# A two-layer hybrid decoder step with hierarchical experts: the experts' rows scattered through DRAM instead of brought back by matmuls

## The chip, the cores and the metric

One NeuronCore of a Trainium2 chip runs the whole step. The metric is the device time of one execution in microseconds.

## The reference

288 tokens (256 of a new sequence, 32 of eight running ones) of width 1024 go through two layers. Of each layer the first half (RG-LRU, Conformer convolution and retention groups, an output projection) isn't touched by the change. The second half is the mixture of experts: each token picks one of 4 groups and in it 2 of 8 experts, so 2 of 32 experts, with a gate for each.

```python
def hier_moe(x, wg, bg, we, be, w1, w3, w2):
    ...
    gates = jnp.sum(jax.nn.one_hot(eid, N_EXPERTS) * (p_top * pe)[..., None], axis=1)
    def expert(acc, params):
        w1e, w3e, w2e, ge = params
        h = jax.nn.silu(xt @ w1e) * (xt @ w3e)
        return acc + ge[:, None] * (h @ w2e).astype(jnp.float32), None
    y, _ = lax.scan(expert, jnp.zeros((B * T, D), jnp.float32), (w1, w3, w2, gates.T))
```

All is float32. An expert's w1, w3 (1024 x 256) and w2 (256 x 1024) are 1 MB each, so a layer reads 96 MB of expert weights. 288 tokens with 2 experts each make 576 rows of 4 KB.

## The kernel before, in words

Every engine has its own program; semaphores alone order them. The experts of a layer are handled in 16 pairs. Each expert has 64 slots for tokens; a pair fills 128 partitions. Before the experts a routing stage works out, for each slot of each pair, which token sits there (`gidx`), its gate (`sel`) and, as `selu`, the number 2 x token + choice; an empty slot has a number past the bound. More tokens than 64 for one expert would go to overflow blocks behind the stage (the `If(n > 0)` parts).

**Weights.** `ring` has 12 places of 1 MB, three (w1, w3, w2) for each of four experts, that is for two pairs. SP issues the loads: `expert` (L473, w1, and L474, w3) once the up projection of the expert two pairs back is done, `expert2` (L478, w2) once the down projection two pairs back is done. The last expert of a layer has places of its own (`spare_w1` and so on, L516 and L521), filled ahead of the stage. SP's instructions go in order, and its loads share one DMA queue.

**A pair on TensorE** (`experts4`): `up` (L918) of the first expert, 32 matmuls into one bank; `turn_h` (L570), two transposes of the hidden rows that ACT has copied out; `up` and `turn_h` of the second; `tokens` (L570), eight transposes of the gathered rows of the next pair; `down` (L944), 16 matmuls into the two banks y0 and y1. ACT makes the tanh and, in `results` (L1850), takes y0 and y1 out, scaled by the gates, into `ysb`. DVE multiplies the hidden values (L1551, L1553) and applies the norm's weights to the turned tokens (L1543).

**Way back.** The rows in `ysb` belong to tokens all over x. POOL builds a matrix of zeros and ones (`back`, L1969), DVE splits `ysb` into three bfloat16 parts (L1561, L1564), and TensorE multiplies: `give_back` (L957, L966, L972) has five parts, two halves of each of the two 128-token tiles and one of the 32 samples, in banks 6 and 7. DVE adds each to x (L1573, L1577). This is done for every pair, between the steps of the next one. For the last pair it stands behind the stage, and then x's norm starts the next layer (or the final norm).

**Gathers.** POOL fetches the token rows of pair g + 1 from the DRAM copy `xn_scratch` by an indirect DMA (L1960) into one of two buffers, once the transposes have read the one before; rows past the bound are skipped.

**Next layer.** SP loads w_in (L493) into the ring's places as the last pairs free them.

## Time and profile before

| | us |
|---|---|
| median of 3 runs | 947.17 |
| lowest, highest | 943.45, 955.58 |
| the profiled execution's own time | 946.95 |
| its span | 945.1 |
| TensorE busy in it | 871.9 (92%) |
| DVE, ACT, POOL busy | 538.7, 173.5, 133.2 |
| DMA moved | 252.79 MB |

The profile is of one execution, in microseconds from the start of its span. A pair of experts takes 15.69 us; the expert stage of layer 0 lies between about 210 and 471 us, that of layer 1 between about 677 and 938 us. PE is TensorE's matmuls, PEld its weight loads. SPq and ACTq are DMA issues of these engines.

### The profile page before, as it was taken

To read this page: it belongs to the slowest core of one execution; us is meant where nothing else is said; L and a number is where in the kernel's file an instruction comes from. 1 tells how busy PE (TensorE), PEld (TensorE's weight loads), DVE (VectorE), ACT (ScalarE), POOL (GpSimd) and SP (SyncE) were. 2 spreads that over 40 slices of the span, in tenths; PEclk is the share of its full clock that TensorE was granted. 3 is DMA by queue.
4 is the path that set the end of the run, shared out by engine and by line. 5 is a ranking of instruction groups with operands and counts; after the bars stand their busy time and mean duration, and the time that the engine had idled before them with its cause. 6 is when DMAs were issued, how large, how long until landed. Compare 5 with 4: busy or idle time off the path is not lost.

```text
span 945.1 us, 14840 instructions
## 1 busy us (share of the span) xinstructions
PE 871.9 (92%) x5548; PEld 493.5 (52%) x5580; DVE 538.7 (57%) x1205; ACT 173.5 (18%) x357; POOL 133.2 (14%) x217
## 2 busy tenths in 40 slices
PE   7999969979999999999799996998799999999994
PEld 6744524575555555555376444336655555555551
DVE  2378794362656565656625787834445555555556
ACT  2213111101211111111301221212012111111113
POOL 0101120031212121211010001200411212121100
PEclk9999979999999999999999998799999999999998
DMA  9953704368999999992953055225499999999911
GB/s 294 309 204 135 232 22 130 133 220 351 409 383 414 404 409 402 419 409 115 345 190 133 1 226 134 89 51 226 162 395 394 418 414 418 407 406 387 391 69 51
DMA packets 100881, 252.79 MB, mean 267 GB/s; under 512 B 31682, under 2 KB 65494, under 8 KB 84438
## 3 DMA queue, kind: packets, MB, share of 16 engines
q1 hardware_dynamic: 73502, 239.45, 65.8%
q10 hardware_dynamic: 22728, 8.02, 3.7%
q0 software_dynamic: 4608, 4.73, 1.6%
q8 instruction: 28, 0.46, 0.2%
q14 instruction: 15, 0.12, 0.0%
HBM read 258.13 MB, written 6.52 MB: 280 GB/s over the span
## 4 chain that ended last, share of the span: by engine, by line
PE 73%; issue 14%; DVE 7%; ACTq 2%; DMA 1%; POOL 1%; ACT 1%; DVEq 0%; SPq 0%; POOLq 0%
PE psum L918 24%; PE psum L944 12%; PE psum L639 10%; PE psum L618 7%; PE psum L570 5%; PE psum L972 4%; PE psum L966 3%; DVE x L1573 3%; ACTq L1783 2%; DVE cb L1193 2%; PE psum L957 2%; PE psum L650 1%; PE psum L576 1%; DMA rows<-xn_scratch,sg 1%; PE psum L713 1%
## 5 line engine op out<-in xcount | busy, mean ns | idle before, releaser
L918 PE MATMUL psum<-ring,arena 128*64 128x256 f32 x1984 | 229.5, 384 | 2.4 <-DVE arena L1543 2.4
L918 PEld LDWEIGHTS psum<-ring,arena 128*64 128x64 f32 x1984 | 143.0, 138 | 87.4 <-issue 25.9
L1573 DVE TENSOR_TENSOR x<-x,psum 128x512 f32<-128x512 f32 x128 | 82.2, 684 | 160.6 <-PE psum L972 160.4
L944 PE MATMUL psum<-ring,arena 128*64 128x512 f32 x496 | 116.8, 598 | 2.4 <-DVE arena L1553 2.4
L639 PE MATMUL psum<-ring,uT 128*128 128x512 f32 x256 | 114.4, 601 | 0.0
L1969 POOL TENSOR_SCALAR kT<-const,sg 128x128 bf16<-128x128 f32 (+1 forms) x96 | 49.2, 522 | 360.9 <-PE psum L957 360.7
L639 PEld LDWEIGHTS psum<-ring,uT 128*128 128x128 f32 x256 | 48.6, 193 | 56.6 <-issue 55.5
L1561 DVE TENSOR_TENSOR v<-arena 128x512 f32<-128x512 f32 x64 | 44.3, 692 | 45.8 <-ACT arena L1850 45.7
L1850 ACT ACTIVATE arena<-psum,sg 128x512 f32<-128x512 f32 x64 | 44.0, 687 | 136.4 <-PE psum L944 136.4
L1857 ACT ACTIVATE arena<-psum 128x256 f32<-128x256 f32 x64 | 24.5, 383 | 238.2 <-PE psum L918 238.2
L944 PEld LDWEIGHTS psum<-ring,arena 128*64 128x64 f32 x496 | 34.2, 136 | 60.7 <-issue 57.3
L618 PE MATMUL psum<-uT,ring 128*128 128x288 f32 x256 | 63.1, 407 | 1.0 <-DVE uT L1118 1.0
L831 PE MATMUL psum<-ring,mixT 128*128 128x512 f32 x128 | 59.5, 620 | 3.3 <-DVE mixT L1409 3.2
L570 PE MATMUL psum<-const,rows 128*128 128x128 f32 (+1 forms) x352 | 49.4, 284 | 9.2 <-DMA rows<-xn_scratch,sg 4.6
L618 PEld LDWEIGHTS psum<-uT,ring 128*128 128x128 f32 x256 | 48.2, 190 | 14.2 <-DVE uT L1118 1.3
L1193 DVE SCALAR_TENSOR_TENSOR cb<-glp,prm,cb 128x256 f32<-128x256 f32 x120 | 54.8, 531 | 0.5 <-DVE hst L1322 0.4
L1577 DVE TENSOR_TENSOR x<-x,psum 32x256 f32<-32x256 f32 x128 | 52.9, 413 | 1.5 <-issue 0.2
L570 PEld LDWEIGHTS psum<-const,rows 128*128 128x128 f32 (+1 forms) x352 | 42.6, 193 | 18.4 <-issue 7.1
L972 PE MATMUL psum<-v,kT 128*128 128x512 bf16 x128 | 49.5, 387 | 1.9 <-DVE kT L1564 1.9
L972 PE MATMUL psum<-kT 128*128 128x512 bf16 x128 | 48.3, 377 | 0.0
L1543 DVE TENSOR_TENSOR arena<-psum,gff 128x512 f32<-128x512 f32 x64 | 41.2, 686 | 12.0 <-PE psum L570 11.1
L576 PE MATMUL psum<-const 128*128 128x128 f32 x282 | 37.8, 299 | 6.9 <-DMA const<-in_constants 4.6
(279 smaller groups left out, 872.1 us busy)
## 6 DMA issues: line engine op xcount, KB each, us to landing
ring<-in_moe_w SPq DMA_DIRECT2D x186, 1024.0 KB, 9.4
ring<-in_w_in SPq DMA_DIRECT2D x24, 1024.0 KB, 11.9
ring<-in_w_out SPq DMA_DIRECT2D x8, 1024.0 KB, 6.4
arena<-in_state_ret ACTq DMA_DIRECT2D x16, 128.0 KB, 8.4
out<-arena ACTq DMA_DIRECT2D x16, 128.0 KB, 2.5
xn_scratch<-rows ACTq DMA_DIRECT2D x4, 512.0 KB, 5.8
uT<-in_moe_w SPq DMA_DIRECT2D x2, 1024.0 KB, 9.8
mixT<-in_moe_w SPq DMA_DIRECT2D x2, 1024.0 KB, 12.7
```

Of the source, the lines that this page charges most:

```text
L570: return pe.transpose(out, in_, ident[0:n, 0:n])
L576: pe.matmul(b[:, 0:128], ident, ident)
L618: i = pe.matmul(b, w[:, k, 128 * (c % 2):128 * (c % 2) + 128], uTk[:, k, :], start=k == 0, stop=k == KT - 1)
L639: i = pe.matmul(b, uTk[:, k, 128 * t:128 * t + 128], w[:, :, k, :], start=k == 0, stop=k == KT - 1)
L831: i = pe.matmul(b, mixT[:, k, 128 * t:128 * t + 128], w[:, :, k, :], start=n_ == 0, stop=n_ == KT - 1)
L918: i = pe.matmul(b[64 * j:64 * j + 64, 0:FE], xsT[:, u // 2, k, s], w[j][:, k, :], start=k == 0, stop=k == KT - 1, skip_group_check=True)
L944: i = pe.matmul(b[64 * q:64 * q + 64, :], hT[:, q, f, :], w[:, 512 * j:512 * j + 512], start=f == 0, stop=f == 1, skip_group_check=True)
L972: i = pe.matmul(b, back[:, pair, 64 * (a - a % 2):64 * (a - a % 2) + 128], y[:, 512 * (a % 2):512 * (a % 2) + 512], start=False, stop=y is ...
L1193: chain[c] = own(STT(dst, glp[:, c, k:k + SEQ], w, dst, ALU.mult, ALU.add))
L1573: i = T(s, s, psum[:, b, :], ALU.add)
L1577: i = T(s, s, psum[32 * q:32 * q + 32, b, 0:256], ALU.add)
L1969: own(pool.tensor_scalar(back[:, g % 2, o:o + n], C("iota")[:, 0:n], tok[:, t, g:g + 1], None, ALU.is_equal))
```

## The change

Let g be the pair's number, 0 to 15.

- The rows of pairs 0 to 13 (`VIA_DRAM`) are written by an indirect DMA from POOL (`scatter`) to `y_dram`, a DRAM scratch of 576 rows, row 2 x token + choice; empty slots are skipped. The scratch is zeroed in each layer by one DMA from SP, whose source is one 512-column row on 64 partitions that POOL has set to zero, read 18 times each.
- When all 14 scatters have landed, SP reads the scratch back in three DMAs (2.36 MB in all) into places 9 to 11 of the ring, both rows of a token side by side. POOL adds the two rows, DVE adds the sum to x (`sums`).
- Pairs 14 and 15 go by `give_back` still, but both accumulate in the same five banks (6, 7, 0, 1, 2), and DVE adds them once at the end (`given_back`).
- On TensorE the down projection of pair g - 1 stands behind the first up projection of pair g (`experts2`); ACT takes its results out there, after waiting for the scatter of pair g - 2 to have landed, since `ysb` is one buffer.
- SP issues the w2 loads of pair p - 1 between the w1 and w3 loads of the two experts of pair p, after a wait for the down projection of pair p - 3. Places 9 to 11 are given to the next layer's w_in only after DVE's sums.
- POOL issues gather g + 2 and then scatter g.

```diff
+VIA_DRAM = NPAIR - 2
...
-EXPERT_TURN = [2, 2, 4, 4, 2, 2, 6, 4]
-PER_BANK = [n + GROUPS * k for n, k in zip(PER_BANK, EXPERT_TURN)]
+EXPERT_TURN = [2, 2, 4, 4, 2, 2, 0, 0]
+BACK_BANK = [6, 7, 0, 1, 2]
+PER_BANK = [n + GROUPS * k + BACK_BANK.count(b) for b, (n, k) in enumerate(zip(PER_BANK, EXPERT_TURN))]
...
+    y_dram = nc.dram_tensor("y_scratch", (2 * NT, D), F32, kind="Internal").ap()
...
+                        if g >= 9:
+                            sp.wait_ge(sums_added, 3 * (l - 1) + g - 8)
+                        elif g % 3 == 2:
+                            xfull(sp, "y1", g // 6, GROUPS - 1, l - 1)
                         else:
-                            xfull(sp, "h", g // 3, last_turn, l - 1)
+                            xfull(sp, "h", g // 3, GROUPS - 1, l - 1)
                     elif g == 10:
...
                     sp.dma_start(spare_w2[f], w2[l, NE - 1, 128 * f:128 * f + 128, :]).then_inc(spare2_in, 16)
-                for it in range(1, GROUPS):
-                    for pair in range(2):
-
-                        experts = [u for u in (2 * pair, 2 * pair + 1) if 4 * it + u < NE - 1]
-                        for u in experts:
-                            xfull(sp, "h", u, it - 1, l)
-                            expert(l, it, u)
-                        xfull(sp, "y1", pair, it - 1, l)
...
+                    pair, it = pair_of(p)
+                    a, b = 2 * pair, 2 * pair + 1
+                    xfull(sp, "h", a, it - 1, l)
+                    expert(l, it, a)
+                    if p > 2:
+                        xfull(sp, "y1", *pair_of(p - 3), l)
+                        late = pair_of(p - 1)
+                        for u in (2 * late[0], 2 * late[0] + 1):
+                            expert2(l, late[1], u)
+                    if 4 * it + b < NE - 1:
+                        xfull(sp, "h", b, it - 1, l)
+                        expert(l, it, b)
+                xfull(sp, "y1", *pair_of(NPAIR - 3), l)
+                expert2(l, GROUPS - 1, 2)
+
+                sp.wait_ge(scattered, 16 * VIA_DRAM * (l + 1))
+                for t, (o, n) in enumerate(TILES):
+                    sp.dma_start(ring[0:n, 9 + t, :].rearrange("p (k d) -> p k d", k=2),
+                                 y_dram.rearrange("(t k) d -> t k d", k=2)[o:o + n]).then_inc(sums_in[t], 16)
                 sp.wait_ge(idx_ready, l + 1)
...
+                def give_back(last, parts):
+
+                    turn_ = 2 * l + last
...
-                def experts4(it, first=False, last=False):
-                    for pair in range(2):
-                        before = (0, it) if pair else (1, it - 1)
-                        up(2 * pair, it)
-                        if pair or not first:
-                            give_back(*before, (0, 1))
-                        turn_h(2 * pair, it)
-                        up(2 * pair + 1, it, spare=last and pair == 1)
-                        if pair or not first:
-                            give_back(*before, (2, 3))
-                        turn_h(2 * pair + 1, it)
-                        if pair or not first:
-                            give_back(*before, (4,))
-                        if not (pair and last):
-                            tokens(pair + 1, it)
-                        down(pair, it, spare=last and pair == 1)
+                    for j in {a % 2 for a in parts if a < 2}:
+                        xfreed(pe, f"y{j}", last, GROUPS - 1, l)
+                    if not last:
+                        for a in parts:
+                            b, n = back_job(a, l)
+                            pe.wait_ge(bank_free[b], n)
+                    for n_, y in enumerate((y_top, y_mid, y_low)):
+                        for a in parts:
+                            b = psum[:, BACK_BANK[a], :]
+                            flags = dict(start=not last and n_ == 0, stop=last == 1 and n_ == 2, skip_group_check=True)
+                            if n_ == 1 and a < 2:
+                                pe.wait_ge(low_ready, 2 * turn_ + a + 1)
+                            if a < 4:
+                                i = pe.matmul(b, back[:, last, 64 * (a - a % 2):64 * (a - a % 2) + 128],
+                                              y[:, 512 * (a % 2):512 * (a % 2) + 512], **flags)
+                            else:
+                                for q in range(4):
+                                    i = pe.matmul(b[32 * q:32 * q + 32, 0:256], back[:, last, SEQ:NT], y[:, 256 * q:256 * q + 256], **flags)
+                            if last and n_ == 2:
+                                i.then_inc(bank_full[BACK_BANK[a]], 1)
+                    if not last and 4 in parts:
+                        i.then_inc(half_back, 1)
+
+                def experts2(pair, it, first=False):
+
+                    up(2 * pair, it)
+                    if not first:
+                        down(1 - pair, it if pair else it - 1)
+                    turn_h(2 * pair, it)
+                    up(2 * pair + 1, it)
+                    tokens(pair + 1, it)
+                    turn_h(2 * pair + 1, it)
...
-                experts4(0, first=True)
+                experts2(0, 0, first=True)
+                experts2(1, 0)
                 with pe.Fori(1, GROUPS - 1) as it:
-                    experts4(it)
-                experts4(GROUPS - 1, last=True)
+                    experts2(0, it)
+                    experts2(1, it)
+                experts2(0, GROUPS - 1)
+                up(2, GROUPS - 1)
+                down(0, GROUPS - 1)
+                turn_h(2, GROUPS - 1)
+                up(3, GROUPS - 1, spare=True)
+                give_back(0, (0, 1))
+                give_back(0, (2, 3))
+                turn_h(3, GROUPS - 1)
+                give_back(0, (4,))
+                down(1, GROUPS - 1, spare=True)
                 for parts in ((0, 1), (2, 3), (4,)):
-                    give_back(1, GROUPS - 1, parts)
+                    give_back(1, parts)
...
+                def split(last):
+
+                    turn_ = 2 * l + last
                     halves = [slice(0, 512), slice(512, 1024)]
+                    if last:
+                        dve.wait_ge(half_back, l + 1)
...
+                def sums(t):
+
+                    n = TILES[t][1]
+                    dve.wait_ge(sums_ready, 3 * l + t + 1)
+                    T(x[0:n, t, :], x[0:n, t, :], ring[0:n, 9 + t, 0:D], ALU.add).then_inc(sums_added, 1)
+
+                def given_back():
+
+                    dve.wait_ge(sums_added, 3 * l + 3)
+                    for a in range(5):
+                        back_full(dve, a, l)
+                        b = BACK_BANK[a]
...
-                def experts4(it, first=False, last=False):
-                    for pair in range(2):
-                        before = (0, it) if pair else (1, it - 1)
-                        if pair or not first:
-                            split(*before)
-                            given_back(*before, (0, 1))
-                        hidden(2 * pair, it)
-                        if pair or not first:
-                            given_back(*before, (2, 3))
-                        hidden(2 * pair + 1, it)
-                        if pair or not first:
-                            given_back(*before, (4,))
-                        if not (pair and last):
-                            tokens(pair + 1, it)
+                def experts2(pair, it):
+                    hidden(2 * pair, it)
+                    tokens(pair + 1, it)
+                    hidden(2 * pair + 1, it)
...
-                experts4(0, first=True)
-                with dve.Fori(1, GROUPS - 1) as it:
-                    experts4(it)
-                experts4(GROUPS - 1, last=True)
-                split(1, GROUPS - 1)
-                given_back(1, GROUPS - 1, (0, 1, 2, 3, 4))
+                with dve.Fori(0, GROUPS - 1) as it:
+                    experts2(0, it)
+                    experts2(1, it)
+                experts2(0, GROUPS - 1)
+                hidden(2, GROUPS - 1)
+                split(0)
+                hidden(3, GROUPS - 1)
+                for t in range(3):
+                    sums(t)
+                split(1)
+                given_back()
...
-                    act.wait_ge(back_ready, l * NPAIR + 2 * it + pair + 1)
+                    act.wait_ge(gate_set, l * NPAIR + 2 * it + pair + 1)
...
+                def one(u, it, first=False):
+                    b, n = expert_job("h", u, it, l)
+                    act.wait_ge(bank_full[b], n + 1)
+                    A(hsb[:, u % 2, :], psum[:, b, 0:256], ACT.Copy).then_inc(bank_free[b], 1)
+                    if u % 2 == 0 and not first:
+                        before = (1 - u // 2, it if u else it - 1)
+
+                        act.wait_ge(scattered, 16 * (l * VIA_DRAM + 2 * before[1] + before[0]))
+                        results(*before)
+                    if not (first and u == 0):
+                        xfreed(act, "hT", (u - 1) % 4, it if u else it - 1, l)
...
                 with act.Fori(1, GROUPS) as it:
-                    experts4(it)
+                    for u in range(4):
+                        one(u, it)
+                act.wait_ge(half_back, l + 1)
+                results(1, GROUPS - 1)
...
+                full(pool, l, "to2")
+                pool.memset(sg[:, 2, :], 0.0).then_inc(zero_ready, 1)
                 pool.wait_ge(slot_ready, l + 1)
...
+                def gate_of(g):
+                    pool.tensor_copy(gate_col[:, g % 2:g % 2 + 1], sel[:, 1, g:g + 1]).then_inc(gate_set, 1)
+
+                def scatter(g):
+
+                    for j in range(2):
+                        xfreed(pool, f"y{j}", *pair_of(g), l)
+                    if g == 0:
+                        pool.wait_ge(y_zeroed, 16 * (l + 1))
+                    pool.indirect_dma_start(out=y_dram, out_offset=bass.IndirectOffsetOnAxis(ap=selu[:, g:g + 1], axis=0),
+                                            in_=ysb, in_offset=None,
+                                            bounds_check=2 * NT - 1, oob_is_err=False).then_inc(scattered, 16)
+
+                def way_back(last):
                     for t, (o, n) in enumerate(TILES):
-                        own(pool.tensor_scalar(back[:, g % 2, o:o + n], C("iota")[:, 0:n], tok[:, t, g:g + 1], None, ALU.is_equal))
-                    pool.tensor_copy(gate_col[:, g % 2:g % 2 + 1], sel[:, 1, g:g + 1]).then_inc(back_ready, 1)
+                        i = pool.tensor_scalar(back[:, last, o:o + n], C("iota")[:, 0:n], tok[:, t, VIA_DRAM + last:VIA_DRAM + last + 1], None, ALU.is_equal)
+                        i.then_inc(back_ready, 1) if t == 2 else own(i)
                 gather(0)
+                gather(1)
+                pool.wait_ge(tok_ready, l + 1)
+                gate_of(0)
+                gate_of(1)
                 for g in range(NPAIR):
-                    if g + 1 < NPAIR:
-                        gather(g + 1)
-                    if g == 0:
-                        pool.wait_ge(tok_ready, l + 1)
-                    way_back(g)
+                    if g + 2 < NPAIR:
+                        gather(g + 2)
+                    if g < VIA_DRAM:
+                        scatter(g)
+                    else:
+                        way_back(g - VIA_DRAM)
...
+                    if g + 2 < NPAIR:
+                        gate_of(g + 2)
+                for t, (o, n) in enumerate(TILES):
+                    pool.wait_ge(sums_in[t], 16 * (l + 1))
+                    T(ring[0:n, 9 + t, 0:D], ring[0:n, 9 + t, 0:D], ring[0:n, 9 + t, D:2 * D], ALU.add).then_inc(sums_ready, 1)
                 o = O[l]
```

## Rows read from the trace of the kernel before

**Rows 1.** The page: GB/s in 40 slices of the span, and the queue of gathers.

```profile
GB/s 294 309 204 135 232 22 130 133 220 351 409 383 414 404 409 402 419 409 115 345 190 133 1 226 134 89 51 226 162 395 394 418 414 418 407 406 387 391 69 51
...
q0 software_dynamic: 4608, 4.73, 1.6%
```

**Rows 2.** Windows: length, busy time of each engine, granted clock, DMA share, GB/s.

```profile
378.10:393.80 15.70, 15.41 (x117) 8.31 (x116) 8.99 (x18) 2.70 (x6) 2.77 (x5) 1.00 1.01 415
425.20:440.90 15.70, 15.41 (x116) 8.31 (x116) 9.00 (x18) 2.69 (x6) 1.67 (x4) 1.00 0.44 176
457.40:467.60 10.20, 7.19 (x41) 2.38 (x41) 6.86 (x14) 3.81 (x6) 0.00 (x0) 1.00 1.10 350
```

**Rows 3.** The chain of waits over one pair: start us, us, what.

```profile
332.26 0.52 PE psum L957 x12
332.78 1.09 PE psum L570 x8
333.87 3.58 PE psum L944 x16
337.45 3.45 PE psum L918 x32
...
341.08 0.39 PE psum L966
341.46 0.88 PE psum L972 x4
342.35 0.22 PE psum L570 x2
342.56 3.60 PE psum L918 x32
346.17 0.56 PE psum L966 x2
346.73 0.45 PE psum L972 x2
...
347.20 0.70 DVE x L1573
```

**Rows 4.** Issues of L474 (w3): 246 to 253 us, then 403 to 410 us.

```profile
L474 SPq DMA_DIRECT2D ring<-in_moe_w x2: 434/518/602, 247.2 to 252.4; - x2
DMA to landing us min/median/max: 10.2/10.2/10.2
...
L474 SPq DMA_DIRECT2D ring<-in_moe_w x2: 433/433/433, 404.1 to 409.3; - x2
DMA to landing us min/median/max: 12.5/12.5/12.5
```

**Rows 5.** The two w2 issues of L478 between 415 and 417 us.

```profile
L478 SPq DMA_DIRECT2D ring<-in_moe_w x2: 378/425/472, 415.9 to 416.4; - x2
...
DMA to landing us min/median/max: 8.5/9.6/10.6
```

**Rows 6.** SP's last issue of the spare w2 and the first ring load.

```profile
L521 SPq DMA_DIRECT2D kr<-in_moe_w x1: 435/435/435, 211.6 to 211.6; - x1
...
DMA to landing us min/median/max: 3.3/4.1/4.8
...
L473 SPq DMA_DIRECT2D ring<-in_moe_w x1: 327/327/327, 217.2 to 217.2; - x1
...
DMA to landing us min/median/max: 4.8/4.8/4.8
```

**Rows 7.** Timeline at the end of the stage, layer 0: start us, us.

```profile
459.10 0.61 PE L944 MATMUL psum<-ring,arena 128*64 128x512 f32 x1 [0.80 <-DVE arena L1553]
...
469.06 1.70 DVE L1577 TENSOR_TENSOR x<-x,psum 32x256 f32<-32x256 f32 x4
```

**Rows 8.** Gathers (L1960) of 220 to 425 us, and a POOL add.

```profile
DMA to landing us min/median/max: 6.4/7.9/8.5
...
L1911 POOL TENSOR_TENSOR mixT<-mixT,arena 128x576 f32<-128x576 f32 x2 | 2.8, 1398 | 0.2
```

101 lines of the change are left out of this document (40 added, 61 removed).

## The prediction

> **What bounds the kernel now.** I read the page's slices first. The span has two copies (one a layer) of the same shape, and the long flat part of each is the expert stage. There the reader is to see that both sides are full at once. The DMA engines move 383 to 419 GB/s [rows 1]. Next the windows of one pair's length: 15.41 us of TensorE in 15.70, clock 1.00, and a DMA share of 1.01 in the same window (the other eleven of the flat part are alike). In the last pair but one of a layer TensorE is just as full while the DMA share is 0.44 [rows 2]. So TensorE sets the pace and its DMA work is over some 30 us before its own. Then the chain of waits over one pair, from L957 at 332.26 us to the add that ends at 347.90, where the next L957 follows: all TensorE but for one 0.70 us add [rows 3]. Ten pairs lie between the w3 load at 247.2 and the one at 404.1 us [rows 4], so a pair is 15.69 us. TensorE never waits for a weight.
>
> The question is how much room the DMA has below TensorE. Two transfers issued back to back land 2.5 us apart (415.9 + 8.5 and 416.4 + 10.6 us) [rows 5]; one is 1 MB, a pair is six of them, so 15.1 us. But the time from issue to landing grows: a w3 load takes 10.2 us at 247 to 252 us and 12.5 us ten pairs later [rows 4]. That is 2.3 us in ten pairs: a pair's DMA takes 15.69 + 0.2 = 15.9 us, more than TensorE's pair. The kernel before is already bound by DMA in rate; it doesn't show because the ring is two pairs deep and the stage ends first. The 0.8 us above 15.1 is what one row gather costs the stream.
>
> **The change, part by part** (in layer 0; layer 1 repeats it).
>
> 1. TensorE loses the give-back of pairs 0 to 13. In the chain that is 0.52 (L957), 0.18 of issue before 341.08, 0.39, 0.88, 0.56, 0.45 and the 0.70 add, 3.68 us; within the add one 0.35 us turn runs, which stays. So 3.3 us a pair, and TensorE's pair would be 12.4 us [rows 3]. If TensorE alone counted that is 14 x 3.3 = 46 us a layer. The extra bubbles are covered: the second turn waits for a copy that the 1.09 us of token turns hides, and the down projection, one pair late, stands where the give-back stood.
>
> 2. What is late next: the weight stream. It takes at least 15.9 us a pair and TensorE now 12.4, so TensorE eats its two-pair lead by about pair 6 and then waits for every transfer. The gain is then not 3.3 us a pair but the lead: TensorE ends right after the stream instead of two pairs behind it. I work the end out from the landing of the last transfer, w2 of expert 30, called E. Before, the w2 issued at 416.4 lands at 427.0; two transfers follow, and a queued third makes 427.0 + 3 x 2.5 = 434.5 us [rows 5].
>
> 3. Scatters. Thirteen lie ahead of E. No row shows one; the nearest is the gather, the same rows of 4 KB (4.73 MB in 32, 36 rows each) on the same queue [rows 1], at 0.8 us each of the stream. Below: nothing, if reading SBUF goes beside the writing that the weights do. Above: 1.6 us, twice the gather, if writes to DRAM hold an engine longer. I take the gather's own price: 13 x 0.8 = 10.4 us (0 to 20.8).
>
> 4. Zeroing. 2.36 MB, at 0.41 MB/us 5.8 us. It is issued behind the spare w2 at about 212 us, which lands by 211.6 + 4.8 = 216.4 us; the first ring load is issued at 217.2 and lands in 4.8 us, so its data would begin near 219.5 [rows 6]. The zeroing ends near 220.5: 1 us late (0 to 2.7). The memset that feeds it falls in an idle stretch of POOL.
> The Trainium skill (SBUF — State Buffer, "Door 1: The DMA port swizzle") says that partitions 0 to 63 reach only 8 of the 16 DMA ports, 218 GB/s at most. The source is just those 64 partitions; by that the zeroing would be an estimated 10.8 us, not 5.8. No row here shows such a transfer at size; it is a rival below.
>
> 5. Waits added. ACT waits for scatter g-1 before it writes the result of g; queued behind it are the tanh of the next expert and so the next down projection. A scatter is issued some 3 us after the down projection ends and, like a gather, should land in 7.9 us (6.4 to 8.5) [rows 8]: 11 us against a pair of 12.4 at first and over 16 later. Covered, by 1.4 us at worst. On POOL the gather of g+3 stands behind the scatter of g, still more than a pair before use: nothing. On SP a w2 load now waits for a down projection before the next w1 load goes out; each comes 3.6 us after the one before, with 20 us of transfers queued: nothing. DVE loses its adds and splits; it wasn't the bound: nothing.
>
> 6. Read-back, seen from E. The last scatter follows pair 13's down projection. Seven transfers follow that pair's w2, so its w2 lands at E - 17.5; the projection takes 3.6, the copies and the issue 2, the scatter 7.9: E - 4. The 2.36 MB read-back queues behind the weights and lands from E + 2.5 to E + 5.8. POOL adds 1024 columns for each of three tiles: 1.40 us for 576 [rows 8], so 2.5 us, and the third ends at E + 10.1. DVE's last add (0.70 us for 512 columns) ends at E + 11.5. The split behind it needs pair 15's first half, at E + 9.2 + 2.7 = E + 11.9. Hidden, with 0.4 us to spare.
>
> 7. The end. w2 of pair 14 lands at E - 2.5. Then: down 3.6, turn 0.35, up of the spare expert 3.6, four give-backs 2.5, turn 0.35, the small give-back 0.5, and 0.8 us for the last hidden values (the 0.80 us idle ahead of 459.10 us [rows 7]). The last down projection starts at E + 9.2. Before it starts at 459.10 and the last add ends at 469.06 + 1.70 = 470.8 us [rows 7]. That tail stays, less some 0.7 us of bank waits which the five separate banks do away with. So a layer gains 459.1 - 9.2 + 0.7 - E = 450.6 - E.
>
> **Sum.** E = 434.5 + 10.4 + 1.0 = 445.9 us; a layer gains 4.7 us, two gain 9.4 us. The profiled execution of 946.95 us (span 945.1) becomes 937.5 us; it lies 0.2 us from the median of the runs shown. The 92 us that TensorE loses in work almost all become waiting.
>
> **Rivals.**
> A. The scatters are nearly free. For it: the two directions may not compete, and the window with a gather in it still reaches 415 GB/s [rows 2]. Against: the gather's 0.8 us is twice what its 0.15 MB would take, so it looks like a price per descriptor. At no cost E = 435.5, 15.1 us a layer, 917 us; at half 927 us.
> B. The zeroing goes at half rate. E = 450.8 us, gain nothing: 947 us. A mechanism of this kernel: a slow transfer stands ahead of the first loads in a stream that never recovers a microsecond. For it stands the rule of the Trainium skill named above; against it, nothing in the rows.
> C. The read-back chain ends late. A scatter that needs 8 us more to land than a gather eats the 0.4 us to spare and puts some 7 us a layer on the end: 951 us. Against: it is the gather's rows and queue, and a gather never took over 8.5 us [rows 8].
> D. Slower than before: scatter writes hold the saturated engines. It decides from (450.6 - 435.5) / 13 = 1.16 us for each scatter. At 1.6 us E = 456.3, a layer loses 5.7, 958 us. For it: the DMA has no slack at all in this stage [rows 4]. Against: the same bytes and count as a gather.
> E. DMA isn't the bound, and its landing times grew only since TensorE left them room. Then 14 x 3.3 x 2 = 92 us go: 855 us. Against: a share of 1.01 with 410 GB/s.
> That the change doesn't do what it says isn't one: the give-backs are gone from the loop in the diff.
>
> **How the numbers follow.** Forecast 0.48, A 0.20, B 0.13, C 0.07, D 0.09, E 0.03. The time is the forecast's, 937.5 us. The range runs from A with no scatter cost (917) to a little past D (962). Faster by over 2% (about what a measurement of this kernel can tell from no change; under 928 us) takes A, nearly all, and E: 0.21. Slower by over 2% needs D with B or worse: 0.07. The rest, 0.72.
>
> **What would show it.** Right: in the pair windows of the middle of the stage TensorE's busy time falls to some 12 us in a window of over 16, the chain names DMA of the weights ahead of L918 and its down projection from about pair 6 on, the DMA share stays at 1.0 to the last pairs, and the last w2 lands near 446 us. TensorE's waits are pieces of 1 to 2 us, so its clock should stay 1.00 (it does in the tail, at 7.19 us of work in 10.20 [rows 2]). Step 3 is wrong if the stream's pair isn't near 16.7 us; step 4 if the first ring load lands later than some 3 us after its old time; step 6 if DVE waits for POOL in front of the last splits. The whole is wrong if the pair windows run at 12.4 us throughout, or if ACT waits on the scatters.

## The result, and the profile after

The changed kernel takes 963.03 us (median of 4 runs, 954.17 to 968.53), the kernel before 946.41 us (943.45 to 955.58) beside it. The ratio is 1.0126 [1.0081, 1.017]: slower by 1.3%, where 937.5 us and a little faster was forecast. The profiled execution took 968.53 us (span 966.6), the longest of the four, and it was left out of the ratio because its granted clock was lower (0.947 against 0.957 to 0.968). So what is read from it is somewhat large; the ratios of the experiments give the size, the profile the places.

The page after: GB/s in 40 slices, granted clock, the queue of gathers and scatters, the chain, and the zeroing's row (the last number of that row is the time from issue to landing).

```profile
PEclk9999978999999999999889998799999998999997
...
GB/s 298 310 181 152 206 51 97 170 186 317 418 418 415 415 416 415 416 416 265 348 169 131 0 222 131 88 49 270 158 354 417 416 416 418 416 416 416 381 205 50
...
q0 software_dynamic: 8640, 9.11, 2.8%
...
PE 44%; DMA 17%; issue 13%; DVE 11%; SPq 10%; ACTq 3%; ACT 1%; POOL 1%; DVEq 0%; POOLq 0%
DMA ring<-in_moe_w 16%; PE psum L953 11%; PE psum L674 9%; PE psum L979 8%; PE psum L653 7%; SPq L494 4%; SPq L493 3%; SPq L498 3%; PE psum L605 3%; ACTq L1828 2%; PE psum L866 2%; DVE arena L1584 2%; DVE cb L1234 2%; PE psum L685 1%; DVE kT L1607 1%
...
y_scratch<-sg SPq DMA_DIRECT2D x2, 2304.0 KB, 14.8
```

Against [rows 1] the flat part is flatter (415 to 418 GB/s) and the weights' DMA is now 16% of the chain. The gather's queue has nearly doubled, 4.73 to 9.11 MB. Windows of one pair, columns as in [rows 2]:

```profile
221.20:236.90 15.70, 14.42 (x110) 8.94 (x112) 2.92 (x8) 3.17 (x8) 0.38 (x1) 1.00 0.98 300
283.90:299.60 15.70, 13.21 (x88) 6.45 (x83) 0.61 (x3) 2.31 (x5) 2.25 (x3) 0.89 1.02 418
378.10:393.80 15.70, 11.47 (x84) 6.34 (x82) 2.34 (x6) 2.59 (x6) 1.37 (x2) 1.00 1.02 414
425.20:440.90 15.70, 13.26 (x98) 7.66 (x94) 2.35 (x6) 2.71 (x7) 2.25 (x3) 1.00 0.90 368
456.50:472.20 15.70, 10.04 (x60) 4.39 (x60) 9.86 (x8) 1.49 (x4) 7.71 (x3) 0.78 1.03 328
```

The third answers to the first of [rows 2]: TensorE 11.47 us instead of 15.41, at a DMA share of 1.02. That is the forecast's picture. Two rows are not. In the first window the DMA engines are full (0.98) and yet move only 300 GB/s. In the last, DVE is busy 9.86 us and POOL 7.71 us.

I measure the stage from the first up projection (before L918, now L953) to the start of the last down projection (the last x16 piece of L944, now L979, in the chain). The first starts stand in these answers, before and after:

```profile
L918 PE MATMUL psum<-ring,arena x118: 379/379/687, 212.0 to 234.9; 128*64 128x256 f32 x118
```

```profile
L953 PE MATMUL psum<-ring,arena x96: 379/379/634, 215.7 to 231.1; 128*64 128x256 f32 x96
```

Before, that is 212.0 to 459.10 [rows 7], 247.1 us; after, 215.7 to 472.61, 256.9 us. In layer 1 it is 247.3 and 255.0 us. So the stages give 9.8 + 7.7 = 17.5 us of the 21.5 us between the spans; 3.7 us lie ahead of the first stage, and 0.3 us is the rest. The forecast wanted 4.7 us less a layer: 242.4 and 242.6 us.

The zeroing of layer 0 from issue to landing (us), then the end of the stage in the chain of waits (start us, us, what):

```profile
L544 SPq DMA_DIRECT2D y_scratch<-sg x1: 587/587/587, 216.1 to 216.1; - x1
...
DMA to landing us min/median/max: 14.7/14.7/14.7
```

```profile
452.78 3.67 PE psum L979 x16
...
457.97 3.37 DVE v L1604 x2
461.34 5.51 DVE kT L1607 x2
...
466.89 4.02 PE psum L1001 x9
...
472.61 3.67 PE psum L979 x16
476.30 0.69 ACT arena L1895
...
477.02 0.69 DVE v L1604
477.71 1.21 DVE kT L1607 x2
```

The zeroing lands at 230.8 us. The first ring load, issued behind it at 221.1 us, lands 14.3 us later by its completion events, where it took 4.8 us before [rows 6]: 9.5 us of backlog, ahead of a stream that is full for nearly the whole stage. And the split of pair 14 (L1604, L1607) stands in the chain with 3.37 + 5.51 = 8.9 us, where the same lines for pair 15, 19 us later, take 0.69 us for a half of L1604 and 1.21 us for both of L1607. The timelines of DVE and POOL say what was beside it:

```profile
457.89 3.45 DVE L1604 TENSOR_TENSOR v<-arena 128x512 f32<-128x512 f32 x2
461.26 5.57 DVE L1607 TENSOR_TENSOR kT<-v 128x512 bf16<-128x512 f32 x2
```

```profile
458.37 2.43 POOL L2056 TENSOR_TENSOR ring<-ring 128x1024 f32<-128x1024 f32 x1 [11.82 <-DMA ring<-y_scratch]
461.00 5.29 POOL L2056 TENSOR_TENSOR ring<-ring 128x1024 f32<-128x1024 f32 x2 [0.20 <-DMA ring<-y_scratch]
```

POOL's three adds of the read-back lie from 458.37 to 466.29 us, DVE's four split instructions from 457.89 to 466.83: the same stretch. Both were in the forecast, each at its right length (2.5 us an add; 10.1 us after E for the third against a measured 11.1). That they would stretch each other was not. DVE's four halves take 2.6 us alone; here they take 9.0, 6.4 us more, against 7.7 us of POOL's adds. One by one it is plainer: the first half starts ahead of POOL's first add and takes 0.68 us, as it does alone; each of the other three lies beside an add of 2.4 to 2.8 us and takes 2.8 us. TensorE's give-backs (L1001) stand behind them. TensorE had little to do meanwhile, and it runs them at the lower of its two clock levels, 1.2 GHz (a granted clock of 0.50):

```profile
466.90:470.90 4.00, 4.00 (x10) 1.57 (x11) 0.00 (x0) 0.00 (x0) 0.00 (x0) 0.50 1.08 346
```

They take 4.02 us in the chain here, and 2.60 where DVE does the sums (experiment 5 below): over 1 us more that comes with the wait.

### The profile page after: what moved, and what is told of

Same layout as the page of the kernel before. It is cut to its first block, busy times and chain, and to the rows that moved or that the text cites. A ratio compares the mean times of both kernels' runs of the same rounds, so it can differ in the third digit from the quotient of the medians.

```text
span 966.6 us, 12792 instructions
## 1 busy us (share of the span) xinstructions
PE 814.8 (84%) x4908; PEld 470.2 (49%) x4908; DVE 362.5 (37%) x859; ACT 169.9 (18%) x357; POOL 135.8 (14%) x169
## 2 busy tenths in 40 slices
DMA packets 107918, 266.57 MB, mean 276 GB/s; under 512 B 34775, under 2 KB 68587, under 8 KB 90902
## 3 DMA queue, kind: packets, MB, share of 16 engines
q0 software_dynamic: 8640, 9.11, 2.8%
## 4 chain that ended last, share of the span: by engine, by line
PE 44%; DMA 17%; issue 13%; DVE 11%; SPq 10%; ACTq 3%; ACT 1%; POOL 1%; DVEq 0%; POOLq 0%
DMA ring<-in_moe_w 16%; PE psum L953 11%; PE psum L674 9%; PE psum L979 8%; PE psum L653 7%; SPq L494 4%; SPq L493 3%; SPq L498 3%; PE psum L605 3%; ACTq L1828 2%; PE psum L866 2%; DVE arena L1584 2%; DVE cb L1234 2%; PE psum L685 1%; DVE kT L1607 1%
## 5 line engine op out<-in xcount | busy, mean ns | idle before, releaser
L953 PE MATMUL psum<-ring,arena 128*64 128x256 f32 x1984 | 231.2, 386 | 38.5 <-DVE arena L1584 26.1
L953 PEld LDWEIGHTS psum<-ring,arena 128*64 128x64 f32 x1984 | 150.4, 138 | 104.8 <-issue 39.9
L979 PE MATMUL psum<-ring,arena 128*64 128x512 f32 x496 | 128.2, 648 | 43.8 <-issue 24.9
L1592 DVE SCALAR_TENSOR_TENSOR arena<-arena,psum 128x128 f32<-128x128 f32 x64 | 18.1, 283 | 311.9 <-ACT arena L1910 296.4
L979 PEld LDWEIGHTS psum<-ring,arena 128*64 128x64 f32 x496 | 39.2, 147 | 117.1 <-issue 116.4
L2031 POOL DMA_INDIRECT y_scratch<-arena,sg x28 | 28.3, 1011 | 388.2 <-ACT arena L1895 374.8
L653 PE MATMUL psum<-uT,ring 128*128 128x288 f32 x256 | 66.5, 423 | 1.0 <-DVE uT L1159 1.0
L653 PEld LDWEIGHTS psum<-uT,ring 128*128 128x128 f32 x256 | 50.3, 198 | 15.4 <-DVE uT L1159 1.3
L866 PEld LDWEIGHTS psum<-ring,mixT 128*128 128x128 f32 x128 | 25.7, 205 | 30.7 <-issue 30.1
L611 PEld LDWEIGHTS psum<-const 128*128 128x128 f32 x282 | 34.1, 201 | 8.2 <-DMA const<-in_constants 4.8
L2018 POOL DMA_INDIRECT rows<-xn_scratch,sg x32 | 33.6, 1051 | 17.0 <-PE psum L605 7.0
L1996 POOL TENSOR_TENSOR rows<-v,const 32x512 f32<-32x512 f32 x16 | 19.0, 1205 | 72.4 <-PE psum L741 38.5
```

What stands on the lines that cost most here:

```text
L611: pe.matmul(b[:, 0:128], ident, ident)
L653: i = pe.matmul(b, w[:, k, 128 * (c % 2):128 * (c % 2) + 128], uTk[:, k, :], start=k == 0, stop=k == KT - 1)
L866: i = pe.matmul(b, mixT[:, k, 128 * t:128 * t + 128], w[:, :, k, :], start=n_ == 0, stop=n_ == KT - 1)
L953: i = pe.matmul(b[64 * j:64 * j + 64, 0:FE], xsT[:, u // 2, k, s], w[j][:, k, :], start=k == 0, stop=k == KT - 1, skip_group_check=True)
L979: i = pe.matmul(b[64 * q:64 * q + 64, :], hT[:, q, f, :], w[:, 512 * j:512 * j + 512], start=f == 0, stop=f == 1, skip_group_check=True)
L2018: pool.indirect_dma_start(out=rows[:, g % 2, :], out_offset=None, in_=xn_dram, in_offset=bass.IndirectOffsetOnAxis(ap=gidx[:, g:g + 1], ax ...
```

## The experiments

Theory from here: (1) the zeroing ahead of the stream costs its whole length, at a low rate; (2) POOL's adds stretch DVE's splits on the critical path; (3) the rest of the forecast holds. The rival throughout is that the scatters, their waits or the clock are the cause. Stage lengths are given for layer 0 / layer 1, measured as above.

**1. Zeroing issued early.** The zeroing's DMA moved up to just ahead of SP's wait for the router's `lgT` (some 30 us ahead of the stage).

```diff
                 expert2(l, 0, 3)
+                sp.wait_ge(zero_ready, l + 1)
+                sp.dma_start(y_dram..., bc(sg[0:64, 2:3, :], ...)).then_inc(y_zeroed, 16)

                 full(sp, l, "lgT")
```

> The zeroing DMA is issued ahead of the routing wait, some 25 us before the stage, where the profile of after has the DMA engines half idle. Theory Z (the zeroing delays the whole weight stream by what it hasn't finished when the first ring load is issued: that load landed 14.3 us after its issue instead of 4.8): the first ring load lands in about 5 us again, the last w2 9 us earlier in each layer, and the time falls by 17 to 19 us, to about 945. Theory S (the scatters' share of the saturated stream is the loss): no more than 2 us. Theory C (TensorE waits for DMA, its clock falls to 1.2 GHz, and slower work is the loss): no change.

958.54 us, ratio 1.0094 [1.0059, 1.0128]: not the 945 us that I expected, and by the ratio not clear of the changed kernel's 1.0126. The stage is 250.1 / 248.6 us, shorter by 6.8 / 6.4 us, and the first ring load lands in 4.8 us again. Some 3.4 us of these 13.2 came back ahead of the two stages; the rest of the gap to 945 is that the stages gave 4 to 6 us less than I expected, and that the changed kernel's profile is 5.5 us above its median, so that a gain read against it looks larger than it is. Windows ahead of the stage:

```profile
180.00:196.00 16.00, 13.51 (x122) 10.63 (x112) 8.25 (x33) 4.31 (x10) 0.00 (x0) 0.89 0.88 333
196.00:212.00 16.00, 14.41 (x112) 13.63 (x110) 9.88 (x48) 0.00 (x0) 6.40 (x10) 0.89 1.03 289
```

The DMA engines were not idle there: with the zeroing among the loads of the first experts and the spare ones they are full (1.03) at 289 GB/s, the zeroing takes 23.7 us to land, and the first gather takes 6.25 us in the chain instead of 4.16, so the first tokens come late. The stage starts at 216.9 us and, in layer 1, 222.9 us after the last down projection of layer 0 (220.1 before).

**2. The sums on DVE alone.** POOL's adds are gone; DVE adds both halves itself, tile 0 behind the split, tile 1 behind the last hidden values, tile 2 behind the second split. The zeroing stays ahead of the stream.

```diff
                 split(0)
+                sums(0)
                 hidden(3, GROUPS - 1)
-                for t in range(3):
-                    sums(t)
+                sums(1)
                 split(1)
+                sums(2)
                 given_back()
```

> Of after, only the end: POOL's three adds of the read-back are gone, DVE adds both rows to x itself, one tile behind the first split, one behind the last hidden values, one behind the second split. Theory P (POOL's 1024-column adds hold DVE's splits, which took 3.4 and 5.5 us instead of 1.4 and 1.3): the splits of pair 14 fall back to some 2.8 us together and the last down projection starts 6 us earlier in each layer; DVE's added work gives 1 to 2 us back; 8 to 11 us less in all, about 953. Theory Q (the splits were late because the rows or the read-back landed late): the same time, with DVE's waits in another place. Theory C (clock): no change, or less than 2 us.

955.18 us, ratio 1.0042 [1.001, 1.0074]. The stage is 249.3 / 248.1 us, 7.6 / 7.0 us shorter. DVE's first split is back at 1.28 us for each of its two lines:

```profile
455.87 1.28 DVE L1604 TENSOR_TENSOR v<-arena 128x512 f32<-128x512 f32 x2
457.07 1.28 DVE L1607 TENSOR_TENSOR kT<-v 128x512 bf16<-128x512 f32 x2
```

**3. Bare.** Left out of the computation: zeroing, scatters, read-back and sums; the down projection one pair late, the missing give-backs and the last two pairs by matmul stay. The rows of pairs 0 to 13 never reach x.

```diff
-                sp.dma_start(y_dram..., bc(sg[0:64, 2:3, :], ...)).then_inc(y_zeroed, 16)
...
-                    sp.dma_start(ring[0:n, 9 + t, :]..., y_dram...).then_inc(sums_in[t], 16)
...
-                        scatter(g)
...
-                for t in range(3):
-                    sums(t)
```

> Left out of the computation: the expert rows of pairs 0 to 13 never reach x (no zeroing, no scatters, no read-back, no sums); the weight stream, the gathers and TensorE's order are those of after. The bound of this order. If DMA bounds the stage, the last w2 lands near 217 us after the first ring load is issued (217.3 worked out for before), TensorE still waits for weights from about pair 6 on, and a layer is 15 us shorter than before: 917 us. If DMA isn't the bound, TensorE's 12.4 us a pair would give about 855. If the falling clock is what costs (theory C), it stays over 930, since TensorE waits here as much as in after.

914.27 us, ratio 0.9632 [0.9569, 0.9694], against 917 from the forecast's own terms. The stage is 229.9 us in both layers. A piece of the chain around a down and an up projection, and a pair's window (DMA share 1.02):

```profile
360.18 24.62 DMA ring<-in_moe_w
...
385.14 3.65 PE psum L970 x16
...
389.87 3.67 PE psum L944 x32
```

```profile
378.10:393.80 15.70, 13.39 (x101) 7.70 (x96) 2.35 (x6) 2.81 (x7) 1.21 (x2) 1.00 1.02 416
```

Even with nothing added the stage waits for weights at a share of 1.02: the give-backs of 14 pairs (46 us a layer of TensorE) are worth 17 us a layer and no more.

**4. Both.** Edits 1 and 2 together.

> Both edits together, the early zeroing and DVE's own sums. Theories Z and P together: 27 us less than after, about 935, so faster than the kernel before by about 1%; what is left against the bare order is the scatters' share of the stream, 13 x 0.6 = 8 us a layer. Under theory S it stays over 950.

943.6 us, ratio 0.9951 [0.9912, 0.9989]. The stage is 242.0 / 241.2 us, but between the layers this one loses 7.6 us against the kernel before (last down projection to first up projection 227.7 us): 8 us above what I expected, again ahead of the stage. Not all of that is the zeroing: experiment 1 has it at the same place and 222.9 us there. The part on the clock below shows what else is different.

**5. Zeroing where the DMA is idle.** The slice from 121 us on moves only 51 GB/s in the changed kernel; a free stretch nearer the start of a layer is the one behind the first expert's loads (issued up to 49 us). There the zero source must exist early: partitions 32 to 127 of `sg[:, 2]` are never written, so they are zeroed once and serve both layers. DVE's sums as in 2.

```diff
                 expert2(l, 0, 0)
+                sp.wait_ge(zero_ready, 1)
+                sp.dma_start(y_dram.rearrange(...), bc(sg[32:128, 2:3, :], [96, 12, 512])).then_inc(y_zeroed, 16)
```

> The zeroing moves to a stretch in which the DMA engines stand idle (behind the first expert's loads of the layer, some 48 us into it), from 96 partitions of a tile that is zeroed once; DVE does the sums. Theory (zeroing in front of the stream costs 8.2 us a layer, POOL's adds 7.6, and nothing else is wrong with the change): the stage has the length of the run with both measures, 241 to 242 us from the first up projection to the last down projection, its start is that of the kernel before, and the kernel takes 936 us (934 to 940), 1% below before. Rival (the early zeroing cost nothing of its own at the start of the stage; the loss there is a slower clock that comes with the change): 943 us, like the run with both measures.

939.87 us (9 runs), ratio 0.9909 [0.988, 0.9939]: 0.9% faster than the kernel before. The stage is 240.9 / 239.3 us and starts at 212.8 us. The window that moved 300 GB/s now reads:

```profile
221.20:236.90 15.70, 14.78 (x114) 9.29 (x111) 2.58 (x7) 2.97 (x7) 2.24 (x3) 1.00 0.98 391
```

and the end of the stage in the chain (the last down projection is 9.4 us behind the last w2, which lands at 444.2 us):

```profile
445.82 3.60 PE psum L953 x32
...
449.59 2.60 PE psum L1001 x11
...
453.68 3.67 PE psum L979 x16
```

**6. Zeroing from 128 partitions**, at the changed kernel's own place, all else as changed.

```diff
-                sp.dma_start(y_dram.rearrange("(p r) (h n) -> p (r h) n", p=64, h=2),
-                             bc(sg[0:64, 2:3, :], [64, 2 * 9, 512]))
+                sp.dma_start(y_dram.rearrange("r (h n) -> (r h) n", h=2).rearrange("(p q) n -> p q n", p=128),
+                             bc(sg[:, 2:3, :], [128, 9, 512]))
```

> The changed kernel with the zeroing read from all 128 partitions instead of 64, at the same place. Rule of the 64 partitions (they reach half of the ports): the zeroing lands about 10 us after its issue instead of 14.8, the first ring load about 4.5 us earlier, and each layer is some 4 us shorter: 955 us. Rival (the writes to DRAM or the size of the pieces set the rate): it lands after 14 to 15 us as before and the time stays at 963 us.

958.28 us, ratio 1.0088 [1.0054, 1.0122]; the stage is 250.9 / 248.2 us, 6.0 / 6.8 us shorter. The zeroing:

```profile
L544 SPq DMA_DIRECT2D y_scratch<-sg x1: 587/587/587, 214.6 to 214.6; - x1
...
DMA to landing us min/median/max: 12.4/12.4/12.4
```

The spare w2 ahead of it lands at 221.2 us here and the zeroing at 227.0, 5.8 us apart: 2.36 MB at 0.41 MB/us, the term of step 4. In the changed kernel these are 221.9 and 230.8 us, 8.9 us apart. In layer 1 the two distances are 7.4 and 9.9 us. The windows between the landings, layer 0 and layer 1, first of the changed kernel:

```profile
221.90:230.80 8.90, 7.98 (x71) 5.80 (x72) 2.35 (x6) 0.94 (x3) 0.00 (x0) 1.00 0.99 249
...
697.50:707.40 9.90, 8.45 (x74) 5.74 (x72) 2.35 (x6) 1.32 (x4) 0.00 (x0) 1.00 1.00 236
```

and of this one:

```profile
221.20:227.00 5.80, 4.79 (x44) 3.32 (x42) 2.06 (x5) 0.66 (x2) 0.00 (x0) 1.00 1.06 423
...
688.80:696.20 7.40, 6.49 (x58) 4.51 (x58) 2.34 (x6) 0.94 (x3) 0.00 (x0) 1.00 1.04 397
```

The share is full in all four, and the rate is 236 and 249 GB/s with 64 source partitions and 397 and 423 with 128. The bytes are the same, and so is the number of packets on the two pages (107918); only the number of source partitions differs, and with it how many rows each one writes, so the 64 partitions are why the DMA engines were full at a low rate. The Trainium skill (SBUF — State Buffer, "Door 1: The DMA port swizzle") has the rule, with 218 GB/s for such a source; the trace agrees with its direction, at the 236 and 249 GB/s of the windows. The first ring load still lands 9.9 us after its issue, 5 us late: the other half of the cost is the place. By the ratio, 1.0088 against 1.0126, the gain of this experiment is inside the two intervals; what it shows is the rate.

**7. Without scatters.** The kernel of experiment 5, which the expectations of 7 and 8 call the first kernel, without the scatters and ACT's wait for them; zeroing and read-back stay, so pairs 0 to 13 add zeros.

> The first kernel of this call without its scatters and without ACT's wait for them; the zeroing and the read-back stay, so the rows of pairs 0 to 13 are read back as zeros and never reach x. Theory (a scatter costs the full stream 0.8 us, 13 of them stand ahead of the last weights): the stage is 10.4 us shorter, 231 to 232 us, and the kernel takes 916 us. Rival (the scatters are nearly free and the read-back is what costs): the stage stays at 240 us or more.

922.01 us, ratio 0.9709 [0.9669, 0.9748]. The stage is 230.3 / 229.9 us: 10.6 / 9.4 us shorter than in 5, 0.77 us a scatter over 13, and within 0.4 us of the bare kernel, so the read-back costs nothing. The total is 6 us above what I expected; its stages start later (217.1 us against 212.8, and 223.4 us between the layers against 222.7), in code that is the same as in 5. The granted clock ahead of the stage is lower here, 0.89 against 1.00 from 180 to 212 us, with TensorE busy 28.4 us instead of 25.5.

**8. POOL beside DVE.** Kernel of 5, and POOL does twelve adds of 288 columns on unused data behind the read-back. Nobody waits for them.

```diff
+                for t in range(3):
+                    pool.wait_ge(sums_in[t], 16 * (l + 1))
+                    for j in range(4):
+                        own(T(rs[:, :], rs[:, :], rs[:, :], ALU.add))
+                        own.wait()
```

> The first kernel of this call, and POOL does twelve adds of 288 columns behind the read-back, on data that nobody uses and nobody waits for; DVE's sums and splits are as there. Theory (POOL's adds hold DVE off the SBUF while they run): DVE's splits in that stretch take 3 to 5 us instead of 1.3 and a layer ends some 3 to 7 us later: 942 to 950 us. Rival (the wait for the sums was the cost, not the engines side by side): as the first kernel, 936 us.

943.39 us, ratio 0.9943 [0.9917, 0.9968], inside the theory's 942 to 950 us, where the rival had 936; the stage is 241.8 / 242.5 us. DVE's and POOL's timelines:

```profile
448.32 1.76 DVE L1604 TENSOR_TENSOR v<-arena 128x512 f32<-128x512 f32 x2
450.00 2.22 DVE L1607 TENSOR_TENSOR kT<-v 128x512 bf16<-128x512 f32 x2
```

```profile
448.75 14.43 POOL L2063 TENSOR_TENSOR rs<-rs 128x288 f32<-128x288 f32 x12 [11.75 <-DMA ring<-y_scratch]
```

DVE's four halves take 4.0 us instead of 2.6 (5 has 1.29 and 1.28), though they touch none of POOL's data and wait for none of its semaphores. So it is the two engines side by side. It is weaker than the theory's 3 to 5 us for a line of two, and than with adds of 1024 columns: POOL's adds here take 1.0 us instead of 2.4 to 2.8, and a half beside them 1.15 us instead of 2.8. Both fit with an instruction of the one holding the other up for about its own length. POOL is held up too: its adds beside the splits take 0.99 us, its shortest 0.66. The Trainium skill (SBUF — State Buffer, "Who interferes with whom") says that a DVE `tensor_tensor` with both inputs in SBUF contends with GpSimd's reads; the trace agrees, with these numbers.

**9. The kernel before, once more.**

> The kernel before once more, for its profile alone: how much of the 4 us by which the expert stage of layer 0 starts later in the changed kernel (216 against 212 us) is a spread between profiles. If that start is the same kernel's spread, it may come out anywhere from 212 to 216 us here; if the change causes it, it stays at 212 us. The stage's own length, 247 us, stays in either case.

947.21 us, one run. Its first up projection starts at 214.5 us instead of 212.0, and its stage is 245.6 / 247.2 us:

```profile
L918 PE MATMUL psum<-ring,arena x108: 379/379/431, 214.5 to 234.8; 128*64 128x256 f32 x108
```

So 2.5 of the 3.7 us by which the changed kernel's first stage starts later are within the spread of one kernel. The windows ahead of the stage, first execution and this one, show what goes with the spread, the granted clock (0.99 and 0.89) and TensorE's busy time:

```profile
180.00:212.00 32.00, 24.68 (x212) 22.17 (x200) 18.67 (x81) 3.62 (x7) 8.12 (x13) 0.99 0.70 254
...
180.00:212.00 32.00, 27.48 (x224) 23.97 (x216) 18.09 (x80) 3.93 (x8) 7.68 (x12) 0.89 0.70 252
```

**10. Only the zeroing moved**, as in 5; POOL's adds stay.

> The changed kernel with the zeroing alone moved to the idle stretch; POOL's adds stay. With this the zeroing and the adds are each taken away alone and together. Theory (two costs that add, 8.2 us a layer for the zeroing ahead of the stream and 7.6 us for POOL's adds beside DVE's splits): the stage is 248 to 249 us long, the first ring load lands within 5 us, DVE's splits still take 3 to 5 us for two, and the time is 16 us below the changed kernel, 945 to 949 us, about that of before. Rival (one of the two hides the other, so that one alone gives nothing or all): 955 us or more, or 941 us or less.

950.71 us, ratio 1.0015 [0.998, 1.005]. The stage is 247.9 / 244.8 us, and DVE's splits are long again:

```profile
447.93 3.48 DVE L1604 TENSOR_TENSOR v<-arena 128x512 f32<-128x512 f32 x2
451.33 5.57 DVE L1607 TENSOR_TENSOR kT<-v 128x512 bf16<-128x512 f32 x2
```

The time is 2 us above my range. With 2, 5 and the changed kernel this makes a square, in stage lengths of layer 0 and 1 and in ratios to the kernel before:

| | POOL's adds | DVE's sums |
|---|---|---|
| zeroing ahead of the stream | 256.9 / 255.0; 1.0126 | 249.3 / 248.1; 1.0042 |
| zeroing in the idle stretch | 247.9 / 244.8; 1.0015 | 240.9 / 239.3; 0.9909 |

The zeroing costs 8.4 to 10.2 us a layer by the profiles, and by the ratios 1.1 to 1.3% of 947 us, so 5 to 6 us. The adds cost 5.5 to 7.6 us, by the ratios 0.8 to 1.1%, 4 to 5 us. They add, and neither hides the other. A difference of two ratios is uncertain by some 0.5% (2 us a layer), and the changed kernel's profiled execution was its longest and that of experiment 5 its shortest. So the place and the sign are shown, and of the size that it lies between these.

## Why the prediction was wrong

The sum of the forecast failed at two steps: step 4 priced the zeroing at 1 us where it cost 9.5 us in the first load's landing, and step 6 put POOL's adds at nothing, as hidden, where they held DVE's split up for 6.4 us. In the profiled executions the miss is 968.5 - 937.5 = 31.0 us (25.5 us by the median): 14.5 and 12.4 us in the two stages, 3.7 us ahead of the first, the rest 0.4 us. Of the 14.5 us, the last w2 (E in the forecast) is 5.6 us late against the start of the stage, the last down projection comes 17.4 us behind it instead of 9.2, and the 0.7 us of bank waits are not seen to be gained. Between its first and its last load the stream took 3 us less than forecast, and that hides a part of step 4's error in E.

Step 1, right in the pace, too high in the work. TensorE is busy 11.5 to 13.4 us in the windows of the middle; forecast 12.4. But of the 3.3 us only 2.8 are matmuls, the rest was waiting for the add, so the work that goes is 28 x 2.8 = 78 us and not 92. The bare kernel's page shows it (790.7 us of TensorE against 871.9); the changed kernel's has 814.8 us, since many of the same matmuls ran at a lower clock.

Step 2, right. The weights' DMA is in the chain with 16% and the share is 1.02. Without scatters the stream's pair measures 15.8 us (w1 into the same slot lands at 285.6 and 412.0 us in experiment 7, eight pairs apart), forecast 15.9. The bare stage is 229.9 us; the forecast's terms give 242.4 - 10.4 - 1.0 = 231.0.

Step 3, right in its sum: 0.77 us a scatter on average against 0.8. It isn't spread as the forecast had it: in the middle eight pairs a pair is 16.3 us, not 16.7, 0.5 us more than without; the larger part of the rest falls in the first four pairs. That the average came out so near is partly luck. Rivals A and D fall by this, and rival E by the bare kernel, 914 us.

What steps 2 and 3 both missed is that the stream does not slow down as a whole. The trace has 16 completion events for each transfer, as many as there are DMA engines. Before the stream is deep they lie within 0.5 us of each other (experiment 7, first ring load, 226.7 to 227.2 us). Then they drift apart: the w1 that lands at 285.6 us has its first event at 282.9, and the one that lands at 412.0 has it at 404.7. So the first parts keep a pace of 15.2 us a pair and the last ones of 15.8. In the changed kernel it is 15.2 and 16.3 us (290.7 to 412.6 us, and 296.9 to 427.6): here a scatter costs the early parts nothing and the late ones 0.5 us. A load has landed only with its last part, so the late parts set the stream's pace, and near its end the engines that are ahead run out of work while those behind still move weights. The DMA's busy tenths from 425 to 460 us of the changed kernel, in 40 slices, fall from 435 us on, though the last w2 lands at 455.2 (the nines from 442 us are its first parts, those from 452 us the read-back):

```profile
DMA  9999999999997876543999963222174999999489
```

So the share did not stay at 1.0 to the last pairs. The drift is there with gathers alone (bare kernel: 15.2 and 15.8 us). Which engines fall behind, and why, no run shows.

Step 4, wrong, and the larger of the two errors. "1 us late (0 to 2.7)" was 9.5 us. It has two causes: I let the zeroing run at 0.41 MB/us, where with its 64 source partitions it took 8.9 us; and I let it begin at once behind its issue, in a gap of 3 us, though the spare w2 ahead of it landed only at 221.9 us. Experiment 6 mends the first and leaves 5 us of the second. Rival B had this mechanism, with 10.8 us for the transfer and 947 us for the kernel. It came true as far as it goes, with a chance of 0.13, but it explains 10 of the 25.5 us; the rest needs step 6. The rule that spoke for it stood in the text with nothing in the rows against it; the chance should have been larger.

Step 5, right. The scatters land in 7.3 to 8.6 us, as in this answer, and ACT is not seen waiting for them:

```profile
L2031 POOL DMA_INDIRECT y_scratch<-arena,sg x14: 1002/1010/1017, 236.5 to 442.3; - x14
...
DMA to landing us min/median/max: 7.3/7.8/8.6
```

SP's issues do block now (L493, L494 and L498 with 10% of the chain), but the loads behind them land 23 to 26 us after issue, so the queue is never empty.

Step 6, right in its times and wrong in its conclusion. The last w2 lands at E = 455.2 us; POOL's third add was to end at E + 10.1 and ended at E + 11.1. "Hidden" was argued from who waits for whom, and POOL's adds hold nobody by a semaphore. They held DVE's split of pair 14, on which the give-backs and the last down projection hang. Experiments 2, 8 and 10 show it, 4 to 7 us a layer. No rival had it: rival C named the same stretch, but for a scatter that lands late, and the scatters landed as forecast.

Step 7, right without the adds: from E to the last down projection is 9.4 us in experiment 5, forecast 9.2, and 17.4 us in the changed kernel.

The clock: "it should stay 1.00" is wrong. It is 0.89 over the pair window 283.90:299.60 in the middle and 0.78 in the tail. In both TensorE has idle pieces (13.21 and 10.04 us busy of 15.70), but so it has in 378.10:393.80, at 11.47 us and a clock of 1.00; the rows don't say which idle piece brings a fall. It falls to the lower of the two levels, 1.2 GHz; the down projection at 420.35 us, with a mean clock of 0.68, takes 5.35 us in the chain instead of 3.65. While the weights are the limit that is hidden. In the tail it is not (the give-backs above, 4.02 us instead of 2.60), and between the layers it isn't either. These are the windows from the last down projection of layer 0 to the first up projection of layer 1, the same code but for the zeroing and the sums, in the bare kernel, the kernel before and experiment 4:

```profile
443.06:660.30 217.24, 192.26 (x977) 114.05 (x979) 128.56 (x314) 40.45 (x77) 25.19 (x32) 0.96 0.47 154
...
459.10:679.20 220.10, 195.89 (x976) 114.65 (x977) 130.55 (x318) 40.65 (x77) 26.36 (x33) 0.95 0.44 147
...
456.93:684.60 227.67, 199.56 (x975) 117.76 (x977) 133.62 (x318) 40.43 (x77) 25.49 (x32) 0.92 0.49 160
```

Over all twelve profiles the length of this stretch goes with its clock: 217.2 us at 0.96, 219.0 to 221.1 at 0.95, 220.7 to 222.9 at 0.94, 222.7 and 223.4 at 0.93, 227.7 at 0.92, with nearly the same number of matmuls. So part of what came out above my expectations in experiments 4 and 7 goes with the clock outside the stage. That is a correlation; why the clock differs there between kernels with nearly the same code, and even between two executions of one, no run shows.

Not tried, and only an estimate: scattering only as many pairs as bring TensorE's end to the stream's. From 247.1 - 3.3 k = 229.9 + 0.8 k that would be some 4 of the 14 pairs, and a stage of about 234 us, 6 us shorter than in experiment 5. It needs the old give-back for the others, with its banks.

## What to carry to other kernels

Before work is taken off a full engine, price what is added to the engine that will be full next: here 46 us of TensorE's path a layer bought 17 us, and the scatters (10), the zeroing (5 to 9) and the sums (4 to 7) took more than that back. A one-off transfer belongs in a stretch where the profile shows the DMA idle, not in a gap next to a saturated stream, and should read from all the partitions it can. A load is there when its last part is: look at the spread of a transfer's completion events, not only at the mean share. And work is hidden beside other work only if the two engines may run side by side: where POOL's adds and DVE's lie in one stretch, count them one after the other.

## What was unexpected in the hardware

- A DMA share of 0.99 to 1.06 does not mean full rate: it moved 236 and 249 GB/s while a 64-partition source was read and 397 and 423 GB/s with a 128-partition one.
- The 16 parts of a transfer drift apart in a full stream with gathers and scatters in it: the last w2 of the changed kernel (issued at 440.8 us) had twelve parts in by 446.5 us, the first at 445.5, and the other four from 449.9 to 455.2.
- DVE `tensor_tensor` of 512 columns takes 0.68 us alone, 2.8 us beside one of POOL's adds of 1024 columns (2.4 to 2.8 us) and 1.15 us beside adds of 288 columns (1.0 us).
- 2.36 MB of zeros issued at 49 us took 17.9 us to land (the median of both layers, experiment 5), and with them at that place the stretch between the layers was 219.6 us (experiment 10) against 220.1 before, so no cost shows; issued 30 us ahead of the stage they took 23.7 us and the first gather 2 us longer.
